# Order of the turns in the mix-out stage, and banks for the last retention tiles, in a two-layer retention and convolution backbone

## The reference, cut to what matters

```python
p = modulate(x, sh1, sc1) @ w_in[l]                 # 3072 columns: q, k, v, g, a, b
o_f, _ = retention_scan(q, k, v, lg_f, s_f)          # 8 heads, chunks of 128 tokens
o_b, _ = retention_scan(flip_seq(q), flip_seq(k), flip_seq(v), lg_b, s_b)
mix_x = mixer_output(o_f + flip_seq(o_b), p, ...)
x = layer_norm(ALPHA * x + g1 * mix_x, ln1_w[l], ln1_b[l])
x = mlp_sublayer(x, sh2, sc2, g2, w_ff1[l], w_ff2[l], ln2_w[l], ln2_b[l])

def mixer_output(o_ret, p, ...):
    ret = silu(g) * (group_norm_per_head(o_ret) * gn_w + gn_b)      # 512 columns
    u = depthwise_conv31(a * sigmoid(b)) + conv_b
    conv = silu(layer_norm(u, cln_w, cln_b))                         # 512 columns
    return concatenate([ret, conv]) @ w_out
```

## Time and profile before

| what | us |
|---|---|
| median of three executions (lowest, highest) | 3000.43 (2994.2, 3005.81) |
| the profiled execution, its own time | 3006.06 |
| its span in the trace | 3004.4 |
| PE busy | 2749.7 (92%) |
| DVE busy | 2084.5 (69%) |
| POOL busy | 989.1 (33%) |
| ACT busy | 717.1 (24%) |

### The profile page before, as it was taken

The page is one execution under the profiler, slowest core; times in us unless marked ns, Lnnn a source line. Parts: engine busy times, 40 slices in busy tenths (PEclk is TensorE's granted clock), DMA queues, the critical chain, the costliest instruction groups (busy, mean ns, idle before and its releaser), DMA issues.

```text
span 3004.4 us, 37044 instructions
## 1 busy us (share of the span) xinstructions
PE 2749.7 (92%) x13212; PEld 2235.7 (74%) x13212; DVE 2084.5 (69%) x3479; ACT 717.1 (24%) x1454; POOL 989.1 (33%) x941
## 2 busy tenths in 40 slices
PE   5999898688999999999999599998588999999995
PEld 3777776477788888888887487786477888888884
DVE  4777785657677667667768788763656767776777
ACT  3222234433211110110111323334423111111111
POOL 1243354456111111111112544453662121212225
PEclk9999999799999999999999799999798999999998
DMA  8222222441122222222220212111422111111111
GB/s 239 87 82 64 85 85 76 135 127 36 50 71 73 70 81 70 70 78 76 70 42 23 95 44 60 58 49 53 135 63 71 42 56 42 54 44 49 49 48 57
DMA packets 246651, 214.60 MB, mean 71 GB/s; under 512 B 60384, under 2 KB 203280, under 8 KB 246544
## 3 DMA queue, kind: packets, MB, share of 16 engines
q10 hardware_dynamic: 139776, 117.46, 13.0%
q1 hardware_dynamic: 106768, 95.77, 10.5%
HBM read 190.56 MB, written 22.63 MB: 71 GB/s over the span
## 4 chain that ended last, share of the span: by engine, by line
PE 79%; DVE 9%; POOL 4%; DMA 3%; ACT 2%; issue 2%; SPq 1%; ACTq 0%; POOLq 0%; DVEq 0%
PE bank L525 14%; PE bank L527 14%; PE bank L526 14%; PE bank L1012 9%; PE bank L1013 9%; PE bank L1014 9%; PE bank L886 2%; PE bank L887 2%; PE bank L888 2%; PE bank L605 1%; PE bank L946 1%; PE bank L945 1%; DVE x_hl L1463 1%; PE bank L929 1%; DVE x_hl L1461 1%
## 5 line engine op out<-in xcount | busy, mean ns | idle before, releaser
L1426 POOL TENSOR_TENSOR w_lo<-raw,w_hi 128x1024 fp32r<-128x1024 f32 x120 | 288.5, 2405 | 1196.4 <-ACT w_hi L1271 1196.4
L1012 PE MATMUL bank<-x_hl,w_hi 128*128 128x512 f32 (+1 forms) x1280 | 475.6, 372 | 0.0
L1013 PE MATMUL bank<-x_hl,w_hi 128*128 128x512 f32 (+1 forms) x1280 | 473.5, 370 | 0.0
L1014 PE MATMUL bank<-x_hl,w_lo 128*128 128x512 f32 (+1 forms) x1280 | 473.1, 370 | 0.0
L525 PE MATMUL bank<-w_hi,h_hi 128*128 128x512 f32 x1152 | 451.5, 392 | 9.8 <-DVE work L1698 7.9
L526 PE MATMUL bank<-w_lo,h_hi 128*128 128x512 f32 x1152 | 449.5, 390 | 0.0
L527 PE MATMUL bank<-w_hi,h_lo 128*128 128x512 f32 x1152 | 449.4, 390 | 0.0
L1675 DVE TENSOR_TENSOR work<-work 128x512 f32<-128x512 f32 (+1 forms) x160 | 147.9, 924 | 428.9 <-ACT work L1262 428.9
L1599 DVE SCALAR_TENSOR_TENSOR bank<-work,bank 128x512 f32<-128x512 f32 (+1 forms) x580 | 407.2, 702 | 18.9
L1698 DVE TENSOR_TENSOR work<-work,bank 128x512 f32<-128x512 f32 x576 | 396.1, 688 | 19.6
L1696 DVE TENSOR_TENSOR bank<-bank,work 128x512 f32<-128x512 f32 x576 | 398.5, 692 | 0.2
(11 more groups left out here) (140 smaller groups left out, 4335.3 us busy)
## 6 DMA issues: line engine op xcount, KB each, us to landing
raw<-in_w_ff ACTq DMA_DIRECT2D x128, 512.0 KB
work<-in_w_ada SPq DMA_DIRECT2D x48, 512.0 KB
raw<-in_w_in ACTq DMA_DIRECT2D x64, 256.0 KB
plain_words<-in_w_ada ACTq DMA_DIRECT2D x64, 256.0 KB
raw<-in_w_in ACTq DMA_DIRECT2D x16, 512.0 KB
plain_words<-in_w_ada SPq DMA_DIRECT2D x16, 512.0 KB, 12.1
raw<-in_w_out ACTq DMA_DIRECT2D x16, 512.0 KB
gate_rows<-work SPq DMA_DIRECT2D x72, 64.0 KB, 1.6
```

Of the source, the lines that this page charges most:

```text
L1012: nc.tensor.matmul(o, slot(mlp_slot(l, f), 0)[:, wc], x_hi[:, k, cols], start=k == 0, stop=False)
L1013: nc.tensor.matmul(o, slot(mlp_slot(l, f), 0)[:, wc], x_lo[:, k, cols], start=False, stop=False)
L1014: mm = nc.tensor.matmul(o, slot(mlp_slot(l, f), 1)[:, wc], x_hi[:, k, cols], start=False, stop=k == KT - 1)
L1426: nc.gpsimd.tensor_tensor(slot(mlp_slot(l, sl), 1), raw[:, un % 2, :], slot(mlp_slot(l, sl), 0).bitcast(F32), ALU.subtract).then_inc(w_rea ...
```

## The change

Three edits, in both layers.

1. DVE's turn of mix-out is now: combine tile st-4, centre and convolution statistics of tile st, low half of tile st-2, variance of tile st, and last scale the heads of tile st-1. The first tile's variance and scaling are done before tile 1 is centred.
2. ACT's turn is now: swish and high half of tile st-2, square of tile st, normalisation of tile st-1, and last the gate swish of tile st-1 (no longer of tile st).
3. The late tiles alternate banks: scores in banks 0 and 1, values in banks 2 and 3. A product then waits for the tile before the last one, and once for all projections to be read out and the convolution to be done.

```diff
         else:
+            late = n > len(steps) + 1
             following = [x for x in ready if x not in scored][:1]
             for x in following:
-                plan.append(("scores", *x))
+                plan.append(("scores", *x, late))
...
+        def ps_scores(r, late):
+            return (banks[r % 2] if late else banks[5])[:, 0:2 * P]
+        def ps_values(r, late):
+            return banks[2 + r % 2] if late else banks[6]
...
                         pe.wait_ge(S["qd_done"], s0["qd_done"] + r + 1)
-                        if r:
+                        if late:
+                            pe.wait_ge(S["evac_q"], s0["evac_q"] + n * PAIRS)
+                            pe.wait_ge(S["prob_done"], s0["prob_done"] + r - 1)
+                        elif r:
                             pe.wait_ge(S["prob_done"], s0["prob_done"] + r)
...
-                        if r:
+                        ps_o = ps_values(r, late)
+                        if late:
+                            pe.wait_ge(S["evac_q"], s0["evac_q"] + n * PAIRS)
+                            pe.wait_ge(S["conv_op"], s0["conv_op"] + 4 * TAPS * len(chunks_of(l)))
+                            pe.wait_ge(S["comb_b"], s0["comb_b"] + r - 1)
+                        elif r:
                             pe.wait_ge(S["comb_b"], s0["comb_b"] + r)
...
                 for st in range(n + 2):
-                    if st < n:
-                        act.wait_ge(S["g_in"][st % 2], s0["g_in"] + 16 * (st // 2 + 1))
-                        nc.scalar.activation(g_in[:, st % 2, :], g_in[:, st % 2, :], ACT.Silu).then_inc(S["silu_g"], 1)
-                        act.wait_ge(S["gn_cent"], s0["gn_cent"] + st + 1)
...
                     j = st - 2
                     if j >= 0:
                         act.wait_ge(S["mixtr_done"], s0["mixtr_done"] + j + 1)
...
                         last.then_inc(S["mix_hi"], 1)
+                    if st < n:
+                        act.wait_ge(S["gn_cent"], s0["gn_cent"] + st + 1)
...
+                        nc.scalar.activation(sq, X[:, T[st], 0:512], ACT.Square).then_inc(S["sq_done"], 1)
+                    j = st - 1
+                    if 0 <= j < n:
...
+                        act.wait_ge(S["g_in"][j % 2], s0["g_in"] + 16 * (j // 2 + 1))
+                        nc.scalar.activation(g_in[:, j % 2, :], g_in[:, j % 2, :], ACT.Silu).then_inc(S["silu_g"], 1)
...
+                centre(0)
+                variance(0)
+                scale_heads(0)
+                for st in range(1, n + 4):
+                    if st >= 4:
+                        combine(st - 4)
                     if st < n:
...
+                        centre(st)
+                    if 2 <= st < n + 2:
+                        low_part(st - 2)
+                    if st < n:
+                        variance(st)
+                    if 2 <= st <= n:
+                        scale_heads(st - 1)
```

More of the change, by code:

```diff
@@ L731, in _ @@
                     if a[0] == "values":
-                        _, p, t = a
+                        _, p, t, late = a
                         r = row_of(l, p, t)
@@ new lines, in combine @@
+                def combine(j):
+                    if j == 0:
+                        dve.wait_ge(S["rows_in"], s0["rows_in"] + 64)
+                    dve.wait_ge(S["z_done"], s0["z_done"] + j + 1)
+                    dve.wait_ge(S["res_in"][j % 2], s0["res_in"] + 16 * (j // 2 + 1))
+                    z = banks[2 + j % 2][:, :]
+                    link(nc.vector.tensor_tensor(z, z, gate_row[:, cond_of(T[j]), :], ALU.mult))
+                    nc.vector.scalar_tensor_tensor(X[:, T[j], 0:512], X[:, T[j], 0:512], ALPHA, z, ALU.mult, ALU.add).then_inc(S["z_read"], 1)
@@ new lines, in low_part @@
+                def low_part(j):
+                    dve.wait_ge(S["mix_hi"], s0["mix_hi"] + j + 1)
+                    cols = slice(T[j] * P, (T[j] + 1) * P)
+                    for half in range(2):
+                        last = nc.vector.tensor_tensor(x_lo[:, 4 * half:4 * half + 4, cols], banks[half][:, :].rearrange("p (a b) -> p a b", b=P),
+                                                       x_hi[:, 4 * half:4 * half + 4, cols].bitcast(F32), ALU.subtract)
+                    last.then_inc(S["mix_lo"], 1)
```

91 lines of the change are left out of this document (35 added, 56 removed).

## The result

| | median us | executions |
|---|---|---|
| before | 3000.72 (2994.2 to 3005.81) | 5 |
| after | 3027.73 (3025.08 to 3030.14) | 5 |

The ratio is 1.0091, interval 1.0077 to 1.0105: the changed kernel is 27 us slower. Its median is 3027.73 us, where 3028 was predicted. The profiled execution of after took 3030.14 us, span 3028.5.

The account below looks back on a forecast made before the run. No engine is full; a loop of waits through several engines sets mix-out's pace. 26.9 + 4.4 + 1.6 - 4.6 = +28.3 us on the median 3000.4 gives 3028.7, stated as 3028, range 3014 to 3041.

Parts of the forecast that it names:

- The loop of 10.67: Mix-out, scaling to next scaling through POOL, PE, ACT and DVE's low half: 10.67 us a turn against 9.44, 1.23 longer.
- The first loops and the last: Mix-out, per layer: two first loops with low-clock transposes at 11.53 us each, a last one without variance at 9.87.
- A sign that was wrong: Mix-out, profile after: POOL's first weighting waits less for the scaling than before (3.33 us), DVE's low half 3 us or more.
- The clock, +4.4: TensorE in mix-out: longer idle time makes 5 of 12 transpose starts slow, 0.88 us each, +4.4 us.
- The end of 10.6: TensorE's clock in mix-out, upper end of the cost: low clock in all 12 loops summed at full clock, +10.6 us.
- DVE beside POOL, +1.6: Mix-out: DVE centres during POOL's operations; the later one waits, mostly DVE; 0.1 us in each of 16 loops, +1.6.
- 26.9: Mix-out of both layers: delay of the last transposes from the longer loops, +14.7 and +12.2 us, passed on in full.
- The late tiles, -4.6: Late tiles: alternating banks bring products to 1.41 us apart from 2.05, store buffers take most back; 2.3 per layer, -4.6.
- The stretched loop with nothing added: Rival, mix-out and late tiles: longer loop without added cost, full gain of the banks; +17, 3017 us, chance 0.13.
- cost in every turn: Rival, mix-out: low clock or port cost in every turn; +40, 3041 us, chance 0.13.
- the shorter turn: Rival, mix-out: scaling doesn't wait for POOL and PE, convolution columns limit a turn to some 8.45; -17, 2984, chance 0.04.
- the cancelled effects: Rival, mix-out and late tiles: the old loop of 9.44 stays the limit, banks give 5; -5, 2995 us, chance 0.06.

Follow-up runs that it names:

- the turns alone: The kernel before with the new DVE and ACT orders of mix-out but the old banks of the late tiles: 3030.63 us, ratio 1.0112 to before.
- the banks alone: The kernel before with only the alternating banks of the late tiles, both mix-out orders old: 2994.78 us, ratio 0.9987 to before.
- Four buffers: The changed kernel with DVE's old order, ACT's square first, and late tiles storing through four buffers instead of two: 2975.16 us, ratio 0.9926 to before.
- the loop was spread over two turns: The changed kernel with DVE's low half back behind the scaling and the square first in ACT's turn: 2982.27 us, ratio 0.9950 to before.

## Why the prediction was right

**The loop of 10.67.** Right in its place and its size: 10.6 us at full clock in after, 9.93 and 9.33 where one link was moved or cut out, and next to no change from the same cut in before (2.4 us, with 0 in the interval). What it didn't say is that the change closed the loop twice, once through DVE's low half and once through ACT's square. The prediction treated the square as covered by DVE's low half; it is, and so undoing DVE's part alone gives back only part (3012, not 2995).

**The first loops and the last.** The first loop took 570.74 - 558.79 = 11.95 in layer 0 against 11.53 counted, the second 11.49. The last took 660.06 - 649.34 = 10.72 with slow transposes, which is the counted 9.87 and a slow start's 0.88.

**A sign that was wrong.** POOL's first weighting was to wait less for the scaling than before. It waited more: 3.1 to 5.4 us in after (5.39 in the turn shown) against 3.33 in the earlier trace rows. The text had POOL late and DVE waiting for it; but in a loop that runs once per turn each engine waits for the rest of the loop, so POOL waits for the scaling all the same. The time doesn't depend on this, since the chain was added up link by link. DVE's low half was to wait 3 us or more and waited 2.0 to 7.2.

**The clock, +4.4.** A little too small. Over the loops behind the first two, the excess of the mixed transposes over 1.09 us adds up to 6.4 us (3.8 and 2.5). Five slow starts in twelve were counted; eight of the twelve had an excess of 0.5 or more, but three of these only 0.5 to 0.7. The end of 10.6 was not reached. The five was a guess from the share of slow gaps, so that it came near is partly luck.

**DVE beside POOL, +1.6.** About right: four of POOL's operations took 1.79 or 1.80 instead of 1.27, 2.1 us in all. But the reason given, that DVE comes later and so waits, is only one side. DVE's small operation L1637 took 0.17 to 0.99 (0.17 in nearly every turn before). The wide one, L1638, went either way. Where it began first, by 0.01 to 0.02 us, POOL's was stretched and it took 0.69 itself; where it began 0.10 and 0.12 us behind POOL's, it took 1.71 and 1.69:

```profile
602.80 0.69 DVE L1638 TENSOR_TENSOR work<-work 128x512 f32<-128x512 f32 x1
...
602.81 1.79 POOL L1396 TENSOR_TENSOR work<-work 128x512 f32<-128x512 f32 x1
...
637.44 1.26 POOL L1396 TENSOR_TENSOR work<-work 128x512 f32<-128x512 f32 x1
...
637.54 1.71 DVE L1638 TENSOR_TENSOR work<-work 128x512 f32<-128x512 f32 x1
```

So the one that began first kept its usual length and the other took longer, as the row of DVE's small operation in the earlier trace rows had shown for one order.

**Mix-out in all.** 26.9 + 4.4 + 1.6 = 32.9 was predicted, 19.0 + 15.3 = 34.3 read from the profile, and 33.6 measured with the turns alone. The clock and POOL were 2.5 us dearer than counted, and the 16 loops some 0.07 us shorter each, which takes back 1.1.

**The late tiles, -4.6.** Right in mechanism, too large: 0.75 + 2.1 = 2.8 in the profile of after, and 3.9 (0.9 to 6.9) measured for the banks alone. Ahead of the row loads the products followed each other in 1.31 to 1.34 us, even closer than the 1.41 counted, but the waits for the stores ate more than was allowed: 2.75 + 1.33 in layer 0 and 2.80 + 1.08 in layer 1. Four buffers brought out what they hid in layer 0.

**The sum.** The two stretches give +31.5, more than the 28.3 of the prediction, and the profiled executions differ by 24.1. The rest, -4.8 ahead of the late tiles of layer 0 and -2.8 behind layer 1's mix-out, with 0.2 between, lies where nothing was changed. Part of it is the choice of execution: before's profiled one lies 5.3 above its median, after's 2.4. So the hit within 1 us is in part luck, with a mix-out 1.4 us too low, late tiles 1.8 us too good, and such scatter on top.

**The rivals.** The stretched loop with nothing added (3017) fell with the slow transposes and with the small gain of the banks; cost in every turn (3041) fell since some starts stay fast; the shorter turn and the cancelled effects fell with a turn over 10.6. The shorter turn came about once the loop was spread over two turns.

## What to carry to other kernels

In a software pipeline written by hand, write down for each cycle through several engines over how many turns it runs, before and after a move. An edit that brings the older tile's step ahead of the newer tile's ends one visible wait, but it may shorten a cycle from two turns to one, and then the whole chain must fit into each turn. To test whether an operation lies on the cycle, cut it out in both kernels: it should move one and not the other.

## What the runs showed of the hardware

- A wide two-input operation of DVE that starts 0.01 us ahead of POOL's makes POOL's take 1.79 to 1.80 us instead of 1.26. It stayed 0.69 itself. The other way round, 0.10 and 0.12 us behind POOL's, DVE's took 1.71 and 1.69.
- Idle time did not settle TensorE's level: the transposes at 638.75 began at full clock after 2.92 us in which PE did nothing, those at 627.27 at the low one after 2.49 and those at 604.66 after 1.33. Eight filler transposes per turn made fast starts more frequent, yet 573.09 and 2149.93 still took 1.97.
- The filler itself, in its first turn, ran at the low level, 1.92 us for eight, and so cost about as much as one slow start of the mixed transposes (0.88): 1.7 us, less the 0.75 and 0.64 by which the transposes right behind it got faster.
